# Walking the tokens in runs of 16 columns in one of three matmuls of a split-precision product

## The chip, the core and the metric

The kernel runs on one core of a Trainium2 chip. The metric is the device time of one execution in microseconds (us); three runs of the kernel before gave 2142.03, 2142.64 and 2142.92 us, a median of 2142.64.

## What is computed

The reference runs 256 tokens of width 1024 through two models in a row, each of two layers, all in fp32. A layer of the first one mixes sliding-window attention, a short convolution and a state-space scan, gates the three and adds them; a layer of the second one gates a retention branch and a second kind of state-space branch. Each layer ends with a gated feed-forward network of 22 x 128 hidden columns. What matters here is that nearly all of the work is products of the 256 tokens with large weight matrices:

```
h = rmsnorm(x, norm_mix[i])
proj = h @ w_in[i]
...
merged = gates[:, :, 0] * y_attn + gates[:, :, 1] * y_conv + gates[:, :, 2] * y_ssm
x = x + merged @ w_mix_o[i]
h = rmsnorm(x, norm_ffn[i])
gt, up = jnp.split(h @ w_ffn_in[i], 2, axis=-1)
x = x + (jax.nn.silu(gt) * up) @ w_ffn_out[i]
```

## The kernel before

**Slabs.** The host cuts all weights into 696 slabs of 128 partitions x 1024 values (512 KB) in the order of their use. Most slabs hold eight blocks of 128 x 128: eight blocks of the contraction for one block of 128 output columns. The activations lie transposed, features on the partitions and the 256 tokens along the row, as a tile of [128, blocks, 256]. So one matmul has a weight block as its stationary operand, 256 tokens as its moving operand, and a [128, 256] fp32 result in one of the four PSUM banks `acc`.

**Split precision.** Each fp32 value is kept as a high part, rounded to the type fp32r, and a low part, the rest. A slab goes through a ring of four slots: the sync engine loads it into `w_raw` (L657), ScalarE rounds it into `w_hi` (`split`, L1325), and VectorE subtracts and writes `w_lo` (L1805). The load of a later slab into a slot waits for the subtraction of the slab that it replaces; ScalarE's rounding waits for the count `used`, by which TensorE says that it is through with a slot. The activations are split in the same way into pairs such as `h_hi`, `h_lo`, or `g`, `f`, `r`, `s`, `m` in the places where other stages make them.

A product of two split matrices takes three matmuls for each block, summed in the same bank: high weights with high activations, high weights with low activations, low weights with high activations. The helper `products` (L762) issues them, on L771, L772 and L773. It is called by `slab_k8` (L819), for a slab of eight blocks with one output block, and by `slabs_long` (L870), for sums that span two or three slabs. The two serve the input projections, the mixers' output projections, and both feed-forward products in all four layers; for the feed-forward input a hardware loop (`ffn`, L894) issues them.

**What goes other ways.** Some slabs don't go through `products`: the first slabs after a normalization (`slab_normed` and `slab_raw`, L784 to L816), slabs of two output blocks (`part_k4`, L835 to L837), three slabs at the start of the mixing product (L857 to L859), the value projection of the second model, with the weights as the moving operand and 512 columns (`slab_rows`, L890 to L892), and the first two slabs in plain fp32 (`slab_direct`, L801). Small fp32 matmuls and transposes of attention, scans and norms (L928 to L1267) run into the banks `mid`, between slabs, in an order that is written out by hand (`ORDER1`, `ORDER2`, `tasks2`).

**Order.** Each engine has its own program, and they meet at counting semaphores. Before a slab TensorE waits for its low weights (`weights_of`) and for its bank to have been read (`bank`). Within `products` there is no wait, but where `need` is given: then one for each block of activations. All tiles of type fp32r begin 16 bytes past a multiple of 32 (`lead=4` in `place`, L327).

Of the kernel before, what the change touches and what calls it, by code (L numbers as in the profile page):

```python
# [321 lines left out]
def hybrid_kernel(nc, weights, x_t, p_d, c1_d, c2_d, decay_d, out_t):  # L322
    with ExitStack() as ctx:
# [402 lines left out]
        def _(pe):  # L726
            mm = nc.tensor.matmul
# [30 lines left out]
            def bank(at, t):  # L758

                pe.wait_ge(out[t % 4], at.four + (t // 4 + 2))  # L760

            def products(at, i, dst, col, width, ks, hi, lo, first=True, last=True, need=None):  # L762


                slot = i % RING
                for j, k in enumerate(ks):
                    if need is not None:
                        need(k)
                    a = j * width + col
                    wh, wl = w_hi[:, slot, a:a + P], w_lo[:, slot, a:a + P]  # L770
                    mm(dst, wh, hi[:, k, :], start=first and j == 0, stop=False)  # L771
                    mm(dst, wh, lo[:, k, :], start=False, stop=False)  # L772
                    done = mm(dst, wl, hi[:, k, :], start=False, stop=last and j == len(ks) - 1)  # L773
                return done

            def slab_normed(at, i, t):
# [42 lines left out]
            def slab_k8(at, i, t, need=None, hi=h_hi, lo=h_lo):  # L819

                weights_of(at, i)
                bank(at, t)
                products(at, i, acc[t % 4][:, 0:T], 0, P, range(KD), hi, lo, need=need).then_inc(used, 1)
# [39 lines left out]
            def slabs_long(at, i, t, n, blocks, hi, lo, need=None):  # L863

                bank(at, t)
                for m in range(n):
                    if at.split + 1 == 2 * DEPTH and t == FO_T2 + KD - 1 and m == n - 1:
                        last_mean(0)
                    weights_of(at, i + m)
                    ks = range(m * KD, min(m * KD + KD, blocks))  # L870
                    products(at, i + m, acc[t % 4][:, 0:T], 0, P, ks, hi, lo, m == 0, m == n - 1, need).then_inc(used, 1)
# [2033 lines left out]
```

## Time and profile before

| | |
|---|---|
| Median of three runs | 2142.64 us (2142.03 to 2142.92) |
| The profiled execution, its own time | 2145.15 us |
| Its span, first to last instruction | 2143.4 us |
| Instructions | 47911, of them 18724 matmuls and as many weight loads |
| Granted TensorE clock, mean | 0.998 |
| Weights and tables read from HBM | 373.14 MB |

The profile gives for each engine when its instructions began and how long each lasted. PE is TensorE's matmul, PEld its weight load, DVE VectorE, ACT ScalarE, POOL GpSimd, SPq the sync engine's queue of transfers. A matmul is written by source line, `out<-in`, and by the size of its operands: `128*128 128x256` is a 128 x 128 weight block and 256 columns on 128 partitions. Records of successive matmuls overlap in time, so the distance from one start to the next tells the rate, and the length of a record does not.

### The profile page before, as it was taken

How to read it: one execution, taken by the hardware profiler on the slowest of the kernel's cores; microseconds unless marked ns; L12 is line 12 of the kernel's file. 1: busy time of each engine (PE TensorE's matmuls, PEld its weight loads, DVE VectorE, ACT ScalarE, POOL GpSimd, SP SyncE). 2: the span in 40 equal slices, each digit the busy share in tenths (PEclk: the TensorE clock that was granted, in tenths of full speed). 3: DMA queues.
4: the chain of work that ended last, by engine and by line, in shares of the span. 5: the costliest groups of instructions: out<-in, count | busy, mean ns of one | idle time of the engine just before them, and what ended most of it. 6: DMA issues, size and time to landing. Idle time of an engine off the chain costs nothing.

```text
span 2143.4 us, 47911 instructions
## 1 busy us (share of the span) xinstructions
PE 2119.0 (99%) x18724; PEld 2061.6 (96%) x18724; DVE 1640.2 (77%) x2626; ACT 1211.6 (57%) x1821; POOL 56.4 (3%) x54
## 2 busy tenths in 40 slices
PE   9999999999999999999999999999999999999998
PEld 8999999999999999899999999999899999999998
DVE  8987877987777776778947877776678947877764
ACT  6646544556555445546658845445546658845443
POOL 0000000000000000000002200000000002200000
PEclk9999999999999999999999999999999999999999
DMA  7434655544446556554544456556554544455553
GB/s 251 158 129 148 202 192 186 197 158 159 139 158 218 186 191 212 179 167 148 174 162 148 148 198 208 185 192 212 181 168 148 177 158 149 151 201 187 186 189 127
DMA packets 102976, 376.54 MB, mean 176 GB/s; under 512 B 11680, under 2 KB 11808, under 8 KB 102304
## 3 DMA queue, kind: packets, MB, share of 16 engines
q1 hardware_dynamic: 101664, 368.66, 51.9%
q10 hardware_dynamic: 1152, 5.58, 0.7%
q8 instruction: 121, 1.98, 0.4%
q14 instruction: 39, 0.32, 0.1%
HBM read 373.14 MB, written 1.05 MB: 175 GB/s over the span
## 4 chain that ended last, share of the span: by engine, by line
PE 90%; DVE 6%; ACT 2%; issue 1%; DMA 0%; DVEq 0%; ACTq 0%
PE acc L771 25%; PE acc L773 24%; PE acc L772 24%; DVE w_lo L1805 2%; PE acc L890 1%; PE acc L891 1%; PE acc L892 1%; PE acc L835 1%; PE acc L837 1%; PE acc L836 1%; ACT w_hi L1325 1%; PE mid L1127 1%; PE mid L1227 1%; DVE pr L2564 0%; PE mid L958 0%
## 5 line engine op out<-in xcount | busy, mean ns | idle before, releaser
L1805 DVE TENSOR_TENSOR w_lo<-w_raw,w_hi 128x1024 fp32r<-128x1024 f32 x694 | 848.0, 1227 | 314.3 <-ACT w_hi L1325 306.2
L1325 ACT CAST w_hi<-w_raw 128x1024 fp32r<-128x1024 f32 x694 | 724.1, 1047 | 534.5 <-PE acc L773 475.0
L771 PE MATMUL acc<-h_hi,w_hi 128*128 128x256 f32 x2096 | 598.1, 285 | 0.3 <-DVE w_lo L1805 0.3
L773 PE MATMUL acc<-h_hi,w_lo 128*128 128x256 f32 x2096 | 586.9, 280 | 0.0
L772 PE MATMUL acc<-h_lo,w_hi 128*128 128x256 f32 x2096 | 585.7, 279 | 0.4 <-issue 0.4
L771 PE MATMUL acc<-g_hi,w_hi 128*128 128x256 f32 x1456 | 409.8, 281 | 0.9 <-DVE w_lo L1805 0.9
L773 PE MATMUL acc<-g_hi,w_lo 128*128 128x256 f32 x1456 | 407.0, 280 | 0.0
L772 PE MATMUL acc<-g_lo,w_hi 128*128 128x256 f32 x1456 | 406.6, 279 | 0.0
L771 PEld LDWEIGHTS acc<-h_hi,w_hi 128*128 128x128 f32 x2096 | 394.9, 188 | 6.6 <-issue 4.7
L772 PEld LDWEIGHTS acc<-h_lo,w_hi 128*128 128x128 f32 x2096 | 394.4, 188 | 1.1 <-issue 0.6
L773 PEld LDWEIGHTS acc<-h_hi,w_lo 128*128 128x128 f32 x2096 | 395.2, 189 | 0.0
L771 PEld LDWEIGHTS acc<-g_hi,w_hi 128*128 128x128 f32 x1456 | 273.8, 188 | 2.0 <-DVE w_lo L1805 1.9
L773 PEld LDWEIGHTS acc<-g_hi,w_lo 128*128 128x128 f32 x1456 | 274.2, 188 | 0.0
L772 PEld LDWEIGHTS acc<-g_lo,w_hi 128*128 128x128 f32 x1456 | 273.3, 188 | 0.2
L771 PE MATMUL acc<-f_hi,w_hi 128*128 128x256 f32 x704 | 197.6, 281 | 0.2 <-DVE w_lo L1805 0.2
L773 PE MATMUL acc<-f_hi,w_lo 128*128 128x256 f32 x704 | 196.8, 280 | 0.0
L772 PE MATMUL acc<-f_lo,w_hi 128*128 128x256 f32 x704 | 196.6, 279 | 0.0
L771 PEld LDWEIGHTS acc<-f_hi,w_hi 128*128 128x128 f32 x704 | 132.4, 188 | 0.4 <-issue 0.4
L773 PEld LDWEIGHTS acc<-f_hi,w_lo 128*128 128x128 f32 x704 | 132.6, 188 | 0.0
L772 PEld LDWEIGHTS acc<-f_lo,w_hi 128*128 128x128 f32 x704 | 132.1, 188 | 0.0
L702 POOL TENSOR_TENSOR sqz<-xs 128x256 f32<-128x256 f32 x32 | 34.0, 1072 | 1808.3 <-DVE xs L2557 1808.0
L2441 DVE SCALAR_TENSOR_TENSOR cv<-acc,p,cv 128x255 f32<-128x255 f32 x144 | 69.2, 481 | 5.5 <-ACT cv L1712 1.8
(438 smaller groups left out, 3438.2 us busy)
## 6 DMA issues: line engine op xcount, KB each, us to landing
w_raw<-weights_d SPq DMA_DIRECT2D x695, 512.0 KB, 3.4
p<-p_d ACTq DMA_DIRECT2D x3, 1080.0 KB, 8.2
rdec<-decay_d ACTq DMA_DIRECT2D x2, 768.0 KB, 6.0
p<-p_d SPq DMA_DIRECT2D x1, 1024.0 KB, 10.9
out_d<-work SPq DMA_DIRECT2D x4, 256.0 KB, 2.3
x_all<-x_d SPq DMA_DIRECT2D x1, 516.0 KB, 4.6
w_raw<-weights_d SPq DMA_DIRECT2D x2, 256.0 KB, 5.8
x_all<-x_d SPq DMA_DIRECT2D x1, 512.0 KB, 6.2
```

The costliest lines, as they stand in the source:

```text
L702: nc.gpsimd.tensor_tensor(sqz[:, b % 4, :], xs[:, b, :], xs[:, b, :], ALU.mult).then_inc(p_zsq, 1)
L771: mm(dst, wh, hi[:, k, :], start=first and j == 0, stop=False)
L772: mm(dst, wh, lo[:, k, :], start=False, stop=False)
L773: done = mm(dst, wl, hi[:, k, :], start=False, stop=last and j == len(ks) - 1)
L835: mm(dst, wh, hi[:, k, :], start=k == 0 and b == 0, stop=False, skip_group_check=True)
L836: mm(dst, wh, lo[:, k, :], start=False, stop=False, skip_group_check=True)
L837: done = mm(dst, wl, hi[:, k, :], start=False, stop=k == 3, skip_group_check=True)
L890: mm(dst, hh, wh, start=k == 0, stop=False)
L891: mm(dst, hh, wl, start=False, stop=False)
L1325: nc.scalar.copy(w_hi[:, slot, :], w_raw[:, slot, :]).then_inc(hi_done, 1)
L1805: tt(w_lo[:, slot, :], w_raw[:, slot, :], w_hi[:, slot, :].bitcast(F32), SUB).then_inc(lo_v, 1)
L2441: op = stt(y[:, j:T], bank[:, 0:T - j], w, y[:, j:T], MUL, ADD)
```

## The change

In the third matmul of `products`, that of low weights and high activations (L773 of the kernel before), both the moving operand and the destination are read and written in another order. The 256 tokens are seen as four quarters (q) of 64, each of four pieces (c) of 16 tokens (e), and the walk takes piece 0 of each of the four quarters, then piece 1 of each, and so on. Moving operand and destination have the same order, so each token's result is added to its own column. The matmuls of L771 and L772, and all those that don't go through `products`, stay as they were, and so do the weight loads and the waits.

```diff
+            def by_quarters(ap):
+
+                return ap.rearrange("p (q c e) -> p c q e", q=4, e=16)
+
             def products(at, i, dst, col, width, ks, hi, lo, first=True, last=True, need=None):
...
                     mm(dst, wh, hi[:, k, :], start=first and j == 0, stop=False)
                     mm(dst, wh, lo[:, k, :], start=False, stop=False)
-                    done = mm(dst, wl, hi[:, k, :], start=False, stop=last and j == len(ks) - 1)
+                    done = mm(by_quarters(dst), wl, by_quarters(hi[:, k, :]), start=False, stop=last and j == len(ks) - 1)
                 return done
```

## Rows read from the trace of the kernel before

**Rows 1.** The page: busy time, share and instructions of each engine.
```profile
PE 2119.0 (99%) x18724; PEld 2061.6 (96%) x18724; DVE 1640.2 (77%) x2626; ACT 1211.6 (57%) x1821; POOL 56.4 (3%) x54
```

**Rows 2.** The page: chain of waits, shares of the span by engine and by line.
```profile
PE 90%; DVE 6%; ACT 2%; issue 1%; DMA 0%; DVEq 0%; ACTq 0%
PE acc L771 25%; PE acc L773 24%; PE acc L772 24%; DVE w_lo L1805 2%; PE acc L890 1%; PE acc L891 1%; PE acc L892 1%; PE acc L835 1%; PE acc L837 1%; PE acc L836 1%; ACT w_hi L1325 1%; PE mid L1127 1%; PE mid L1227 1%; DVE pr L2564 0%; PE mid L958 0%
```

**Rows 3.** Windows: length, busy us and count by engine, clock, DMA share, GB/s.
```profile
620.00:800.00 180.00, 180.00 (x1535) 179.95 (x1534) 139.93 (x219) 85.83 (x112) 0.00 (x0) 1.00 0.59 196
...
1000.00:1070.00 70.00, 70.00 (x589) 69.16 (x588) 62.81 (x113) 48.32 (x82) 0.00 (x0) 1.00 0.47 158
```

**Rows 4.** TensorE in order of time, 1000 to 1004 us: start, length, engine, line.
```profile
1000.10 0.28 PE L773 MATMUL acc<-h_hi,w_lo 128*128 128x256 f32 x1
1000.22 0.28 PE L771 MATMUL acc<-h_hi,w_hi 128*128 128x256 f32 x1
1000.34 0.28 PE L772 MATMUL acc<-h_lo,w_hi 128*128 128x256 f32 x1
...
1003.97 0.28 PE L773 MATMUL acc<-h_hi,w_lo 128*128 128x256 f32 x1
```

**Rows 5.** Groups by line, 620 to 800 us: busy us, mean ns, idle before.
```profile
L1805 DVE TENSOR_TENSOR w_lo<-w_raw,w_hi 128x1024 fp32r<-128x1024 f32 x64 | 78.4, 1225 | 17.7 <-ACT w_hi L1325 16.7
L1325 ACT CAST w_hi<-w_raw 128x1024 fp32r<-128x1024 f32 x65 | 68.0, 1048 | 84.9 <-PE acc L773 65.0 <-PE acc L837 9.5 <-PE acc L859 4.3
```

**Rows 6.** Waits over the span: us in total, times, longest us.
```profile
PE mid L958 <- issue: 2.5, 1, 2.5
PE mid L747 <- POOL zpad L695: 1.7, 1, 1.7
...
PE acc L771 <- DVE w_lo L1805: 1.3, 5, 0.4
...
ACT w_hi L1325 <- PE acc L773: 475.0, 315, 2.2
```

**Rows 7.** Waits of the sync engine's queue, as above.
```profile
SPq L657 <- DVE w_lo L1805: 1672.6, 688, 11.8
```

**Rows 8.** Groups by line and form over the span, line 773 on TensorE.
```profile
L773 PE MATMUL acc<-h_hi,w_lo 128*128 128x256 f32 x2096 | 586.9, 280 | 0.0
...
L773 PE MATMUL acc<-g_hi,w_lo 128*128 128x256 f32 x1456 | 407.0, 280 | 0.0
...
L773 PE MATMUL acc<-f_hi,w_lo 128*128 128x256 f32 x704 | 196.8, 280 | 0.0
...
L773 PE MATMUL acc<-s_hi,w_lo 128*128 128x256 f32 x256 | 71.6, 280 | 0.0
L773 PE MATMUL acc<-r_hi,w_lo 128*128 128x256 f32 x256 | 71.6, 280 | 0.0
...
L773 PE MATMUL acc<-m_hi,w_lo 128*128 128x256 f32 x128 | 35.8, 279 | 0.0
```

**Rows 9.** Line 1186: four matmuls in order of time, and all (ns min/median/max).
```profile
1045.08 0.60 PE L1186 MATMUL mid<-c,xs 128*128 128x128 f32 x4
...
L1186 PE MATMUL mid<-c,xs x64: 270/273/329, 1031.4 to 1717.9; 128*128 128x128 f32 x64
```

**Rows 10.** Line 801, fp32: 20 matmuls in order of time, and its group.
```profile
8.88 4.48 PE L801 MATMUL acc<-xd,w_raw 128*128 128x256 f32 x20
...
L801 PE MATMUL acc<-xd,w_raw 128*128 128x256 f32 x32 | 7.4, 385 | 1.0 <-DMA w_raw<-weights_d 0.8
```

**Rows 11.** TensorE in order of time: matmuls of 512 columns, first and eighth.
```profile
848.27 0.39 PE L891 MATMUL acc<-w_lo,g_hi 128*128 128x512 f32 x1
...
849.88 0.39 PE L892 MATMUL acc<-w_hi,g_lo 128*128 128x512 f32 x1
```

**Rows 12.** All engines in order of time at 700 us: weight loads and matmuls.
```profile
700.21 0.28 PE L771 MATMUL acc<-g_hi,w_hi 128*128 128x256 f32 x1
700.21 0.19 PEld L772 LDWEIGHTS acc<-g_lo,w_hi 128*128 128x128 f32 x1
700.33 0.27 PE L772 MATMUL acc<-g_lo,w_hi 128*128 128x256 f32 x1
```

## The prediction, on record before the change was run

> **What bounds the kernel now.** I read the busy shares first, then the chain of waits, then the groups by line, and last the order of time in a quiet stretch. The shares put TensorE at 99% of the span, with VectorE at 77% and ScalarE at 57% [rows 1]. A busy share of matmuls overstates, because the records overlap: one lasts 0.28 us and the next starts 0.12 us later. So the chain decides: 90% of the 2143.4 us runs through TensorE, and lines 771, 772 and 773 alone are 25 + 24 + 24% of it [rows 2]. In the stretch from 620 to 800 us TensorE was never without a matmul, 1535 of them in 180 us, which is 117.3 ns from one start to the next, at a granted clock of 1.00 [rows 3]. That is the number that everything here hangs on. A second reading of it: from 1000.10 to 1003.97 us lie 33 starts, again 117.3 ns [rows 4]. All three products have the same step.
>
> The other engines wait for TensorE and not the reverse. In the same 180 us VectorE makes the low weights of 64 slabs in 78.4 us and ScalarE the high ones of 65 in 68.0 us, and ScalarE stood idle 65.0 us of it for line 773 [rows 5]. Over the whole span TensorE's own longest waits are 2.5 and 1.7 us, and for the low weights it waited 1.3 us in five places [rows 6]. The sync queue's load of a raw slab waits for VectorE, 1672.6 us in total, so the transfers are paced from behind and are not late [rows 7].
>
> **What the change touches.** Line 773 ran 2096 + 1456 + 704 + 256 + 256 + 128 = 4896 times, once for each triple of the helper [rows 8]. Nothing is added, removed or moved: the same instructions in the same order, with the same weight loads, waits and semaphores, and no DMA. Only the order of the 256 columns within one instruction differs: 16 runs of 16 columns, each run 64 bytes long, the next one 256 bytes further on, and at the end of each four a jump back. Source and destination are permuted alike, so every sum is the same. The whole cost is 4896 times whatever one such instruction gains or loses on the 117.3 ns step, and since TensorE is on the chain with nothing beside it, that product goes to the end time undiminished. One nanosecond is worth 4.9 us, 0.23% of the span. About 0.2%, 4.3 us or 0.9 ns for each changed matmul, is what a measurement of this kernel can tell from no change.
>
> No row of the kernel before has a matmul that walks in runs, so the price must be bounded. The floor: four matmuls of 128 columns on fp32 operands take 0.60 us for the group, of which the last is 0.273; so (0.60 - 0.27) / 3 = 0.11 us from start to start, each with a weight load of 128 columns [rows 9]. The fp32 operands take two passes over the columns by this reading: 20 matmuls of 256 columns take 4.48 us, (4.48 - 0.39) / 19 = 215 ns each, or 108 ns for each 256 column times of one pass [rows 10]. Thus 256 column times can be streamed in 108 to 110 ns, 7 to 9 ns under the 117.3 of the changed kind. At the clock of rows 3, the 2.4 GHz level, 256 columns would be 106.7 ns. If the new walk took all of that loss away, it would gain 4896 x 8.2 ns = 40 us; that is the end of the range on the fast side. The ceiling: reading at half the rate, as rows 10 do per column, 215 ns. This would cost 4896 x 98 ns = 480 us. Between the two lies the price of a hiccup at each run: one cycle of 0.417 ns at 15 breaks is 6.3 ns, or 31 us in all; two cycles are 12.5 ns and 61 us.
>
> Which value? The loss of 10.6 ns over 106.7 is not a fixed cost of changing the weights alone: matmuls of 512 columns step by (849.88 - 848.27) / 7 = 230 ns [rows 11], 16.7 ns over 213.3. So of the loss roughly 5 ns is fixed and 6 ns grows with the columns. Some part of the full-rate fp32r stream stutters already. It does not depend on the neighbours: VectorE is busy for 62.81 of the 70 us from 1000 us on, and for 139.93 of the 180 from 620 us on [rows 3], and the step of rows 4, inside the first of these, is that of the second. A load of weights begins with the matmul before it and lasts 0.19 us by its record, across that matmul's step [rows 12], and it is not touched. The runs are long: 64 bytes, sixteen fp32 values, so that a break is rare against what must be read anyway. An address that jumps once in 16 columns is computed beside the stream if the unit looks even one access ahead, and the record of one matmul, 0.28 us against a step of 0.117, shows more than two of them in flight. I take 0 ns, and keep -8.2 and +6.3 (with a tail above) for the range. Sum: 4896 x 0 = 0; the profiled execution took 2145.15 us beside a span of 2143.4, and the median of the three runs is 2142.64, 2.5 below the profiled one. **Forecast 2142.6 us.**
>
> A rule speaks against this. What the rows show first: the contiguous stream of fp32r costs 117.3 ns where the fp32 passes cost 108 [rows 3, 10]. The Trainium skill (Advanced Engine Details and Errata, section Memory Cachelines) says of PSUM: "Any non-contiguous AP significantly slows down matmuls", and in the next sentence only asks that every two consecutive elements be contiguous; for SBUF it asks for two hits to each line of 16 bytes. By the first sentence the change is a loss of unstated size; by the others runs of sixteen values lose nothing. No row here shows either. I take the milder reading as likelier.
>
> **The rivals.**
>
> *The breaks cost cycles (slower, 0.33).* The place is the column stream of line 773: either the read of the activations or the write into the bank stops for a cycle when a run ends. It decides from 0.9 ns on, that is from about two cycles for each whole matmul. At one cycle for each of 15 breaks: 2142.6 + 31 = 2173. At two: 2204. A variant in the same place: the bank still adds the previous product when the permuted one comes to the same column. Before, 256 columns lie between the two; now column 192 comes 48 columns into the product and the distance is 256 - 192 + 48 = 112 columns, 47 ns at 0.417. It would be felt twice for a triple, entering the permuted walk and leaving it. For this rival: the stream at full rate already shows a part that grows with the columns [rows 3, 11], so it is read near its limit. Against: 64-byte runs, and several matmuls in flight. About 0.08 of the 0.33 goes to the strong form, in which the walk streams towards the half rate of rows 10, up to 2142.6 + 480 = 2623; the Trainium skill's sentence above is this form, and I give it that little because its own next sentence is met.
>
> *The walk removes part of the stutter (faster, 0.22).* If the loss of 6 ns that grows with the columns comes from successive accesses falling on one part of the memory, in the read or in the add, a walk that turns over four quarters could spread them. All of rows 10's difference gone gives 2142.6 - 40 = 2103; half gives 2123. For it: the loss is real, and two kinds of stream show that TensorE can go faster. Against: nothing in the rows ties it to addresses. The three lines have the same step in rows 4, though they read three different tiles. TensorE would not run into the other engines at this gain: a slab of 24 matmuls would shrink from 2.82 to 2.75 us, while VectorE's part is 1.23 and ScalarE's 1.05 [rows 5].
>
> *The change does nothing at all* because the pattern folds back into one run: excluded. The runs of 16 are 64 elements apart, so neither inner pair of dimensions can be merged; and if it did, the number would be that of the forecast.
>
> **How the numbers follow.** No effect within 0.2%: 0.45, at 2142.6, its own range 2138.3 to 2146.9. Slower by over 0.2%: 0.33, at 2173 in the likeliest form. Faster by over 0.2%: 0.22, between 2103 and 2138. As cases of both signs hold more than half, the range reaches to 2104 on the left, leaving out about 0.02, and to 2182 on the right, which takes in one cycle for each break with 9 us for a cost at both ends of the walk, and leaves out the two-cycle case and the strong form, together some 0.14.
>
> **What would show it.** In the changed kernel, the stretch from 620 to 800 us is to hold 1535 matmuls again, within 3 (0.2%), if the forecast is right; about 1508 if each break costs a cycle (the mean step then 119.4 ns); about 1572 if the walk frees 8.2 ns (114.5 ns). In the order of time, the step that follows a start of line 773 is what should move, and those after 771 and 772 should stay; if the distance in the bank is the cause, the step after 772 moves as well. The mean duration of line 773's record, 280 ns now [rows 8], should stay or grow by the cost of its own stream. If the time changes while the step after 773 does not, my whole account of where the change acts is wrong. If the walk in runs costs tens of ns, the wait of ScalarE for line 773 will grow from 475.0 us [rows 6] by as much as the span grows.

## The result, and the profile after

The changed kernel took 2150.28 us, the median of seven runs (2148.34 to 2152.36), and the kernel before 2142.92 in seven runs beside it (2142.03 to 2144.74): a ratio of 1.0032, with a 95% interval of 1.0023 to 1.0041. It is slower by 7.4 us. The forecast was no change, at 2142.6 us.

The lines of `products` are 775, 776 and 777 now, four further down than before. The page of the changed kernel gives the busy shares, the chain by engine and by line, and ScalarE's costliest group with its longest wait; they answer to [rows 1, 2, 6]:

```profile
PE 2124.6 (99%) x18724; PEld 2067.1 (96%) x18724; DVE 1639.9 (76%) x2626; ACT 1212.3 (56%) x1821; POOL 56.4 (3%) x54
...
PE 91%; DVE 5%; ACT 2%; issue 1%; DMA 0%; DVEq 0%; ACTq 0%
PE acc L777 25%; PE acc L775 25%; PE acc L776 25%; DVE w_lo L1809 2%; PE acc L894 1%; PE acc L895 1%; PE acc L896 1%; PE acc L839 1%; PE acc L840 1%; PE acc L841 1%; PE mid L1231 1%; ACT w_hi L1329 1%; PE mid L1131 1%; PE mid L1217 0%; PE mid L962 0%
...
L1329 ACT CAST w_hi<-w_raw 128x1024 fp32r<-128x1024 f32 x694 | 724.3, 1047 | 537.8 <-PE acc L777 482.5
```

The structure is the same. TensorE bounds the kernel as before, VectorE and ScalarE do the same work, and ScalarE waits 7.5 us longer for line 777 than it did for 773 (482.5 against 475.0 us), about what the whole run has gained in length. The windows of the changed kernel (columns as in [rows 3]):

```profile
620.00:800.00 180.00, 180.00 (x1529) 179.95 (x1529) 140.84 (x221) 85.80 (x110) 0.00 (x0) 1.00 0.59 195
...
1000.00:1070.00 70.00, 70.00 (x585) 69.08 (x584) 61.24 (x111) 48.09 (x81) 0.00 (x0) 1.00 0.47 158
```

In 180 us in which TensorE was never without a matmul there are 1529 of them where there were 1535, at the same granted clock. (This view counts every record that touches the window; 1527 and 1532 of them start inside it.) That is about 117.7 ns a step for 117.3. TensorE in order of time, the first and the tenth start of the changed line after 1001 us:

```profile
1001.20 0.28 PE L777 MATMUL acc<-h_hi,w_lo 128*128 128x256 f32 x1
...
1004.38 0.28 PE L777 MATMUL acc<-h_hi,w_lo 128*128 128x256 f32 x1
```

Nine triples in 3.18 us are 353.3 ns each; [rows 4] gives eleven in 3.87 us, 351.8. A triple here is the three products of one block. The traces give starts to the nanosecond. Over all steps from one product to the next that are shorter than 180 ns, the mean step after the first, second and third product was 117.73, 116.55 and 117.70 ns before and is 119.03, 116.59 and 117.84 now. The sum of the differences, 1.48 ns, times 4896 triples is 7.2 us, which accounts for the loss within the scatter of the runs. Most of it is not where I looked for it, after the changed product, but one start later. I take from this that the start of a record doesn't tell when that matmul's columns stream.

In the table, "triple" is the mean time of three steps in one long stretch of 1530 steps without other matmuls, worked out from its starts; in the kernel before it begins at about 667 us. Kernels that read alike give it alike to 0.1 ns, where the time of the whole kernel scatters by some 2 us: 352.0 ns before, 353.4 after. It holds for this stretch and not for every place: taken over all steps as above, all_three has 354.6 ns and the change 353.5, though the stretch gives both the same. At the granted level of 2.4 GHz a column each cycle would be 320.0 ns for the triple. Experiments were compared with runs of the kernel before on the same chip, whose median was 2143.8 to 2144.6 us.

### The profile page after: what moved, and what is told of

The parts are those of the page before. It is cut to its first block, busy times and chain, and to the rows that moved or that the text cites. A ratio compares the mean times of both kernels' runs of the same rounds, so it can differ in the third digit from the quotient of the medians.

```text
span 2149.4 us, 47911 instructions
## 1 busy us (share of the span) xinstructions
PE 2124.6 (99%) x18724; PEld 2067.1 (96%) x18724; DVE 1639.9 (76%) x2626; ACT 1212.3 (56%) x1821; POOL 56.4 (3%) x54
## 4 chain that ended last, share of the span: by engine, by line
PE 91%; DVE 5%; ACT 2%; issue 1%; DMA 0%; DVEq 0%; ACTq 0%
PE acc L777 25%; PE acc L775 25%; PE acc L776 25%; DVE w_lo L1809 2%; PE acc L894 1%; PE acc L895 1%; PE acc L896 1%; PE acc L839 1%; PE acc L840 1%; PE acc L841 1%; PE mid L1231 1%; ACT w_hi L1329 1%; PE mid L1131 1%; PE mid L1217 0%; PE mid L962 0%
## 5 line engine op out<-in xcount | busy, mean ns | idle before, releaser
L1329 ACT CAST w_hi<-w_raw 128x1024 fp32r<-128x1024 f32 x694 | 724.3, 1047 | 537.8 <-PE acc L777 482.5
```

What stands on the lines that cost most here:

```text
L1329: nc.scalar.copy(w_hi[:, slot, :], w_raw[:, slot, :]).then_inc(hi_done, 1)
```

## The experiments

| Kernel | Median us | Ratio (95% interval) | Triple, ns |
|---|---|---|---|
| the change | 2150.3 | 1.0032 (1.0023 to 1.0041) | 353.4 |
| src_only | 2150.4 | 1.0029 (1.0018 to 1.0039) | 353.4 |
| dst_only | 2144.9 | 1.0002 (0.9992 to 1.0011) | 352.0 |
| dst_piece2 | 2145.2 | 1.0000 (0.9991 to 1.0009) | 352.0 |
| all_three | 2155.8 | 1.0050 (1.0033 to 1.0067) | 353.3 |
| first_only | 2139.1 | 0.9975 (0.9966 to 0.9985) | 350.0 |
| piece8 | 2183.3 | 1.0178 (1.0161 to 1.0195) | 360.1 |
| piece4 | 2211.1 | 1.0308 (1.0291 to 1.0325) | 366.7 |
| piece2 | 2865.8 | 1.3368 (1.3346 to 1.3391) | 500.0 |
| piece4_near | 2125.6 | 0.9906 (0.9890 to 0.9921) | 346.7 |
| before_16_down | 2135.3 | 0.9961 (0.9946 to 0.9975) | 350.0 |
| after_16_down | 2146.5 | 1.0015 (1.0005 to 1.0024) | 353.3 |
| weights_16_down | 2162.6 | 1.0082 (1.0069 to 1.0096) | 354.7 |
| still_plain | 2148.4 | 1.0016 (1.0006 to 1.0026) | 353.3 |
| still_quarters | 2134.7 | 0.9956 (0.9939 to 0.9972) | 350.0 |
| moving_still | 2077.8 | 0.9691 (0.9675 to 0.9707) | 335.0 |
| near4_all | 2126.7 | 0.9914 (0.9897 to 0.9930) | 347.3 |
| near4_all_16_down | 2112.5 | 0.9852 (0.9836 to 0.9868) | 344.5 |
| near4_third_16_down | 2123.1 | 0.9900 (0.9883 to 0.9916) | 346.7 |

### Read or write

```diff
# src_only
-                    done = mm(by_quarters(dst), wl, by_quarters(hi[:, k, :]), ...
+                    done = mm(dst, wl, by_quarters(hi[:, k, :]), ...
# dst_only
+                    done = mm(by_quarters(dst), wl, hi[:, k, :], ...
# all_three: by_quarters on operand and destination of all three products
```

> Only the moving operand of the third product is read by quarters; its destination is written in the plain order, so the low-weight product of a token is added to another token's column. Three theories for the 7.4 us that the change cost (2142.9 to 2150.3). Read: the breaks in the stream of the activations cost, so this run keeps the cost, 2149 to 2151 us, and 1529 matmuls start between 620 and 800 us. Write: the breaks in the destination cost, so this run is at 2143 us, with 1535. Join: what costs is that two matmuls in a row come to the same column of the bank 112 columns apart and not 256; the destination is plain here, so 2143 us, with 1535.

> Only the destination of the third product is written by quarters; the activations are read in the plain order (a token's low-weight product again lands in another token's column). Read: 2143 us, 1535 matmuls between 620 and 800 us. Write and join: 2149 to 2151 us, 1529 matmuls.

> All three products of a block are walked by quarters, in operand and destination; the output is that of the reference. Read and write: three times the cost of the change, 2142.9 + 22 = 2165 us, and about 1517 matmuls between 620 and 800 us. Join: the successive matmuls have the same order again, 256 columns apart, and only other work on the bank differs: 2143 to 2144 us, 1535 matmuls.

src_only has all of the cost, dst_only none. The window of 620 to 800 us, first of src_only and then of dst_only:

```profile
620.00:800.00 180.00, 180.00 (x1530) 179.95 (x1529) 140.98 (x221) 86.20 (x112) 0.00 (x0) 1.00 0.60 195
```

```profile
620.00:800.00 180.00, 180.00 (x1534) 179.95 (x1534) 140.43 (x220) 85.69 (x111) 0.00 (x0) 1.00 0.59 196
```

The 1530 steps last 180.211 us in src_only and 180.211 in the changed kernel; 179.520 in dst_only and 179.519 in the kernel before. So the write by quarters costs nothing that can be measured here (the interval is 0.1% to either side), nor do the two accumulations that meet 112 columns apart; it is the read of the activations. The three products together did not cost three times as much: +11.8 us for an expected 22, and in the long stretch the very triple of the change. That was the first sign that the price does not belong to a matmul by itself.

A stronger test of the write, with pieces of 8 bytes in the destination alone (`e=2`, 127 breaks):

> Only the destination of the third product is walked, in pieces of 2 columns, 8 bytes, 127 breaks; its activations are read in the plain order (tokens' low-weight products land in other columns). Operand and destination together cost 722 us in this form. Read theory, as the run with pieces of 16 showed it: the write is free here too, 2143 to 2146 us. If a write in pieces has a price that 64 bytes hid, as the pieces of the read have, it would show: anything from 2150 us up to 2866 us.

Ratio 1.0000, and again the triple of the kernel before. For 64-byte and for 8-byte pieces the write order is free here.

### The length of a piece

The change's `e=16` became 8, 4 and 2 in operand and destination; the four quarters stay, so the jumps stay 256 bytes long.

> As the change, with pieces of 4 columns in place of 16: 63 breaks and not 15 in each of the 4896 matmuls, each piece 16 bytes. If a break has a price (read or write), 63/15 x 7.4 = 31 us, so 2174 us and about 1509 matmuls between 620 and 800 us. If the price is one for each matmul in which the order differs, or for the two changes of order in each triple (join), 2149 to 2151 us and 1529 matmuls.

> Pieces of 8 columns, 31 breaks in each matmul, where the change has 15 and cost 7 us, and pieces of 4 have 63 and cost 67 us. If the price is straight in the breaks from a free allowance on (a small buffer ahead of the array that hides the first ones), the line through the two known points, 1.25 us for each break more, gives 7 + 16 x 1.25 = 27 us: 2171 us. If the price grows with the share of short pieces (pieces of up to some length are free, shorter ones not), it stays near the change's, 2150 to 2155 us.

> Pieces of 2 columns, 8 bytes, 127 breaks, so that each stretch of 16 bytes is fetched twice. Straight in the breaks: 67 + 64 x 1.25 = 147 us, 2291 us. If what counts is the number of 16-byte stretches fetched (64 of them for pieces of 4 and more, 128 here), the step of a permuted matmul rises towards twice its length, 4896 x 100 ns = 490 us: 2630 us.

Breaks (places where one piece ends and the next begins elsewhere) numbered 15, 31, 63 and 127 and cost 7, 39, 67 and 722 us. None of the written expectations gave these numbers: piece4 took 2211 us for 2174 or 2150, piece8 2183 for 2171 or 2150 to 2155, piece2 2866 for 2291 or 2630. Neither the straight line in the breaks nor the free piece length held. piece2 in order of time:

```profile
700.23 0.42 PE L777 MATMUL acc<-h_hi,w_lo 128*128 128x256 f32 x1
700.47 0.31 PE L775 MATMUL acc<-h_hi,w_hi 128*128 128x256 f32 x1
700.61 0.28 PE L776 MATMUL acc<-h_lo,w_hi 128*128 128x256 f32 x1
700.73 0.42 PE L777 MATMUL acc<-h_hi,w_lo 128*128 128x256 f32 x1
```

Here the slow stream is seen: 0.42 us for the record of the changed product, 0.24 to the next start, and some of the delay again after the first product (0.14 or 0.15). A triple lasts 500 ns in place of 352, all of it from one matmul that reads 8 bytes at a place.

### Where the pieces and the tiles lie

```diff
# before_16_down, after_16_down: every tile placed with lead=4, 16 bytes lower
# (all fp32r tiles, and x_all, which these matmuls don't read)
-                return flat[:, lead:].rearrange(...)
+                return flat[:, 0:n // 4 - lead].rearrange(...)
# weights_16_down: the same for w_hi and w_lo alone, in the kernel before
# piece4_near: the third product in pieces of 4, the next one 64 bytes on
-                return ap.rearrange("p (q c e) -> p c q e", q=4, e=16)
+                return ap.rearrange("p (q c e) -> p c q e", q=16, e=4)
# first_only: by_quarters in the first product and not in the third
```

> The kernel before, with every tile of type fp32r placed 16 bytes lower (each has begun 16 bytes past a multiple of 32 until now). The activation tiles then begin at a multiple of 64 bytes. Alignment theory: the unit that reads the moving operand fetches stretches of 32 or 64 bytes, and a tile that begins inside one costs a fetch more for each contiguous run; with one run in each matmul this is at most one fetch in 17 or 33, so 2143 us or a little less. Break theory (only the jumps count, wherever they begin): 2143 us. If the time rises, the offset itself carries a part of the step of 117.3 ns, which neither theory says.

> The changed kernel with the same shift of 16 bytes, so that every piece of 16 columns is one whole stretch of 64 bytes. Alignment theory: the extra fetches are gone, and the time is that of the kernel before with the same shift, within 1 us. Break theory: it stays 6 to 8 us over that kernel.

Both expectations of the first fell: the kernel before gains 8.7 us by the shift (2135.3 against 2144.0 on that chip), with a triple of 350.0 ns. The windows of before_16_down and of after_16_down:

```profile
620.00:800.00 180.00, 180.00 (x1544) 179.95 (x1543) 139.11 (x217) 87.05 (x114) 0.00 (x0) 1.00 0.59 198
```

```profile
620.00:800.00 180.00, 180.00 (x1532) 179.95 (x1531) 139.56 (x220) 87.28 (x114) 0.00 (x0) 1.00 0.58 196
```

And the change costs more there than without the shift: 11 us over the shifted kernel before, 3.3 ns a triple for 1.4. The expectation speaks of activation tiles that begin at a multiple of 64 bytes; by the kernel's addresses that is so of the high ones, while the low ones begin 32 bytes past one. The changed product reads the high ones, so each of its pieces is one whole stretch of 64 bytes after the shift, and it is not a matter of pieces that straddle.

Traffic of the other engines is not it either. In the long stretch of before_16_down the steps repeat in a cycle of six, and each of the six keeps within 1 ns over all 1534 steps after the first, while VectorE is busy for 139 of 180 us.

> The kernel before with only the two weight tiles (high and low) 16 bytes lower; the activations stay. With all fp32r tiles lower the kernel took 2135 us and a step of 116.7 ns in place of 117.3. Theory 1, the weight load's reading depends on where its block begins: the whole gain is here, 2135 us and 1541 matmuls between 620 and 800 us. Theory 2, the moving operand's reading does: nothing is gained here, 2143 us and 1532 to 1535. Theory 3, the two readings get in each other's way and their distance counts: another value, which may lie on either side of both.

> Pieces of 4 columns as in the run that took 2211 us, but with jumps of 64 bytes in place of 256 (sixteen parts of 16 columns, a piece of each in turn). If a break costs because the address leaves the run, whatever the distance, 2211 us and a step of 122.2 ns again. If it costs because of where it lands (the four quarters fall on the same part of the memory, or the near piece has been fetched with its neighbours), it differs: towards 2143 us.

> By quarters in pieces of 16, operand and destination, in the first of the three products and not in the third. The step in the long stretches was 117.8 ns with the third product changed, and 117.8 with all three. If any one permuted read sets this step for the triple, 2150 us and 1527 to 1529 matmuls between 620 and 800 us. If the price hangs on what follows the permuted product (the change of weights from low to high, or none), it differs by some us, and then 2143 us is as possible as 2157.

The outcome of weights_16_down was neither that of theory 1 nor that of theory 2, and first_only came out at neither number written for it. These three turned the question round. The windows of weights_16_down and of piece4_near:

```profile
620.00:800.00 180.00, 180.00 (x1517) 179.95 (x1516) 140.92 (x221) 85.72 (x111) 0.00 (x0) 1.00 0.58 192
```

```profile
620.00:800.00 180.00, 180.00 (x1554) 179.95 (x1553) 141.74 (x221) 87.89 (x114) 0.00 (x0) 1.00 0.61 199
```

The activations are read as before in weights_16_down, and only the address of the weights is another by 16 bytes: 18 us slower. piece4_near has as many breaks as piece4, in pieces of the same 16 bytes, and where piece4 lost 67 us it gains 19. And the very walk of the change, in the first product, gains 5 us. A price per break is refuted, and so is a price of 16-byte pieces as such. What counts is where the read of the activations goes, and where the weights lie. One difference between piece4 and piece4_near besides the length of the jumps is not separated: of the 63 breaks 15 lead back in the first and 3 in the second.

### Still operands

The weight load of the next product runs beside the matmul [rows 12]. If the two reads get in each other's way, taking the movement out of either should tell.

```diff
# still_plain (kernel before) and still_quarters (the change), in products:
-                    wh, wl = w_hi[:, slot, a:a + P], w_lo[:, slot, a:a + P]
+                    wh, wl = (w[:, slot, a:a + 1].to_broadcast([P, P]) for w in (w_hi, w_lo))
# moving_still (kernel before), in all three products
-                    mm(dst, wh, hi[:, k, :], ...
+                    mm(dst, wh, hi[:, k, 0:1].to_broadcast([P, T]), ...
```

> The kernel before, but in all three products of the helper the weight load reads one column of its block 128 times over (a step of zero) and not the 128 columns; so the output of all these slabs is another. It leaves the 256-column read of the activations as it was and takes nearly all movement through memory out of the weight load. Collision theory: the read of the activations and the load of the next weights, which runs beside it, meet in the memory, and this is the part of the step of 117.3 ns over 106.7 to 109; then the step falls to 108 to 110 ns, 14688 x 8 = 117 us, 2026 us. Own-stream theory: the read of the activations has its price by itself, and the step stays at 117.3 ns, 2143 us.

> The changed kernel with the same still weights. Collision theory: the walk in pieces of 16 costs nothing where no moving weight load runs beside it, so the time is that of the plain walk with still weights, within 2 us, and so is the step. Own-stream theory: 6 to 8 us over it, as in the change.

> The other half of the pair: the weight loads of the helper read their real blocks, and all three products read one token's column 256 times over (a step of zero), so that the output of these slabs is another; destinations are plain. If the loss over 106.7 to 109 ns comes from fetching the activations through memory, the step falls to 108 to 110 ns and the time to 2026 us. If it is in the weight load, or in handing over from one to the other, the step stays within 116 to 118 ns, 2125 to 2155 us. With still weights the step was 117.8, so the first outcome would put the loss into the moving operand alone.

The windows of still_plain and of still_quarters:

```profile
620.00:800.00 180.00, 180.00 (x1530) 179.95 (x1530) 140.85 (x221) 85.75 (x110) 0.00 (x0) 1.00 0.60 195
```

```profile
620.00:800.00 180.00, 180.00 (x1542) 179.95 (x1541) 139.18 (x218) 87.40 (x114) 0.00 (x0) 1.00 0.61 198
```

With still weights the step did not fall, and the collision theory as I had put it failed on both numbers: 2148.4 us for 2026, and the quarters not equal to the plain walk but 14 us faster. Own-stream theory failed too, for it wanted the quarters slower. So the effect of the walk changes its sign with the pattern of the weight reads: +7 us with the real weights, -14 us with still ones (triples 352.0 to 353.4, and 353.3 to 350.0). Two separate prices, one for each read, that simply add up can't give this. moving_still, window and order of time:

```profile
620.00:800.00 180.00, 180.00 (x1603) 179.95 (x1603) 140.80 (x221) 93.09 (x123) 0.00 (x0) 1.00 0.63 205
```

```profile
699.96 0.28 PE L775 MATMUL acc<-g_hi,w_hi 128*128 128x256 f32 x1
700.07 0.28 PE L776 MATMUL acc<-g_lo,w_hi 128*128 128x256 f32 x1
700.18 0.28 PE L777 MATMUL acc<-g_hi,w_lo 128*128 128x256 f32 x1
...
700.85 0.28 PE L777 MATMUL acc<-g_hi,w_lo 128*128 128x256 f32 x1
```

Six steps from 700.18 to 700.85 us, 0.112 each. By the long stretch it is 111.7 ns, and all steps are 111 or 112, where they lay between 111 and 125 before. Its fall of 5.7 ns is between the outcomes I had written. So 5.7 of the 10.7 ns over 106.7 go when the activations are no longer fetched as 256 different columns, and the other 5.0 are there without it.

The kernel did not get all of this. Three times 5.7 ns for 4896 triples would be 83 us, and it became 66 us faster. Part of the rest is waiting of TensorE for low weights, which was 1.3 us in five places before [rows 6]:

```profile
PE acc L775 <- DVE w_lo L1809: 7.5, 14, 1.3
```

### Versions that beat both

> Pieces of 4 columns with jumps of 64 bytes, which in the third product took the kernel to 2125.6 us, now in all three products, operand and destination; the output is that of the reference. If each product has its own gain of 18 us, 2090 us. If the step is set by the triple as a whole, as by quarters (117.8 ns with one and with three), 2120 to 2130 us. Collision theory allows a loss as well, since the activations' order is matched to other weight loads.

> The same with every fp32r tile 16 bytes lower, which in the plain order gained 8.4 us. If the two gains are of different kinds they add: 8 us under the run without the shift. If both take away the same collisions, they do not: equal within 2 us, or worse.

> Pieces of 4 columns with jumps of 64 bytes in the third product alone, with every fp32r tile 16 bytes lower; the output is that of the reference. With all three products this way the kernel took 2112.5 us. Without the shift the third alone (2125.6) and all three (2126.7) were equal. If the shift adds to it as it does there, 14 us, 2111 us; if the shift's gain is that of the plain walk, 8 us, 2117 us.

near4_all was as its second guess said: no better than the third product alone. With the shift it went to 2112.5 us, 32 us under the kernel before; its gain and the shift's more than add (18 + 9 against 32), which neither outcome written for it allowed. With the third product alone the shift hardly helps: 2123.1 us for the 2111 or 2117 expected, 21 us under the kernel before where piece4_near without the shift was 19 under, and the triple is the same 346.7 ns. The window of near4_all_16_down:

```profile
620.00:800.00 180.00, 180.00 (x1565) 179.95 (x1564) 139.26 (x218) 89.40 (x119) 0.00 (x0) 1.00 0.61 201
```

## Why the prediction was wrong, point by point

**The frame held.** TensorE's steps set the kernel's time: they lengthened by 7.2 us in sum, and the end came 7.4 us later. TensorE waited no longer for another engine's low weights than before (1.1 us in four places, for 1.3 in five).

**The step that failed** is the choice between the bounds, the price of the walk for each changed matmul: "An address that jumps once in 16 columns is computed beside the stream if the unit looks even one access ahead ... I take 0 ns". The walk cost 1.5 ns for each changed matmul, in the read: 7.2 us where the sum had 4896 x 0. The range held it because it was wide, well under the first rival's 6.3 ns, and the sign was that rival's. But its mechanism was wrong as well: it priced breaks, and 63 breaks can gain 19 us or lose 67, by where they lead. Its variant, the bank's accumulation at 112 columns, fell with dst_only.

**The decomposition agreed with the runs and was not used.** From [rows 11] I had a fixed part of about 5 ns and one that grows with the columns, about 6 ns for 256. moving_still left 5.0 and took away 5.7. That the part which goes with the movement is the part which grows with the columns is likely by this, and not shown. A loss of 6 ns that grows with the columns streamed is one that a new order of them can move, up or down; 0.9 ns was enough to be seen. Having found it I should have taken most of the chance from "same".

**"Nothing in the rows ties it to addresses" was read too strongly.** The three lines having equal steps though they read three tiles was my evidence. But they read two activation tiles, not three (`h_hi`, `h_lo`, `h_hi` in [rows 4]), and their steps were not equal: 117.73, 116.55 and 117.70 ns on average, and between 111 and 125 ns one by one, which rows rounded to 10 ns don't show. Besides, all activation tiles begin at one offset, 16 bytes past a multiple of 32, and their blocks follow in steps of 1024 bytes; the rows could hardly have shown a dependence. A shift of 16 bytes showed it: it gained 8.7 us with all tiles and cost 18 us with the weights alone. The rival of a gain rested on addresses, and addresses do count; that successive accesses fall on one part of the memory, as it had it, is not shown.

**What would show it.** I wanted 1535 starts within 3 in the window, or 1508; there were 1529. I wanted the step after line 773 to move, and wrote that otherwise my account of where the change acts is wrong; of the 1.48 ns only 0.14 came there, and 1.30 after the first product. The account of the place was right all the same, as src_only shows, and the test was wrong. A delay in the stream shows one start later, or there and one later (in piece4 +12.3 ns after the third and +5.5 after the first, with 2.9 less after the second), so what one product costs should be read from the sum of its triple.

**The Trainium skill's rule** (Advanced Engine Details and Errata, section Memory Cachelines). Its sentence on PSUM, that any non-contiguous access pattern slows matmuls significantly, is not what these runs show: with pieces of 8 bytes in the destination the ratio was 1.0000 (0.9991 to 1.0009). Its second sentence, that two neighbours should be contiguous, agrees with that. For SBUF it asks for two hits on each 16-byte line; piece2 has just that in its read, and its triple rose from 352 to 500 ns.

**What stays open.** Shown is that the step depends on the order in which the activations are read and on the address and the pattern of the weight load, and that the effect of the one depends on the other. That the two reads meet in the memory is an inference from this; one run, still_plain, speaks against its simplest form, since still weights left the step at 117.8 ns (though a load that reads one place 128 times is still a read). Why the walk by quarters costs 1.5 ns in the third product and gains in the first stays open. How the memory is divided, so that 64-byte jumps help and 256-byte ones hurt, was not tried, nor were the activations moved by 16 bytes without the weights, nor was there a kernel without weight loads between the products.

## What to carry to other kernels

Where a stream of matmuls runs at its full rate and its step lies some nanoseconds above one column a cycle, the order of the moving operand and the addresses of both operands are knobs worth about a per cent (1.5% at best here): try offsets of 16 bytes and short pieces with near jumps, and expect either sign. The destination has to follow the same walk, or the sums are wrong; that was free in these runs. Price such an edit from the part of the step that grows with the columns, and don't call it free because no wait and no instruction changes. Judge it from the sum of the steps in a stretch without other work, which repeats far better than the kernel's time, and then look at the kernel's time as well, since the stretch can hide a difference elsewhere and part of a gain can go into waits.

## What the runs showed that I had not expected

The steps of the plain walk repeat, within 2 ns, in a cycle of 15 matmuls, from 111 to 125 ns, with a triple of 352.0 ns. Most other triples lie on a grid: 335.0, 346.7, 350.0, 353.3, 360.1, 366.7 and 500.0 ns are all within 0.1 of a multiple of 1.667 ns, and most of these kernels repeat in a short cycle (the change's in 6 matmuls, within 1 ns after the first few); 344.5, 347.3 and 354.7 do not. My guess, untested, is that a small extra stall can be swallowed, or cost a whole notch of this grid; this would be one way for the same walk in one product and in three to give the same triple (353.4 and 353.3). And the order of the columns in one matmul of three, with nothing else changed, spans from 2125.6 to 2865.8 us.
